# RWKV scan on one core: the outputs of two chunk groups move behind the X and Y products of the second and fourth level in TensorE's order

## The chip, the core and the metric

The kernel runs on one core of a Trainium2 chip. The metric is the device time of one execution in microseconds. Five engines work side by side, each through its own queue in program order: TensorE (PE in the rows; PEld are its weight loads), VectorE (DVE), ScalarE (ACT), GpSimd (POOL) and SyncE (SP). They meet through semaphores alone.

## What is computed

The reference is one encoder layer over two batches (1024 and 256 tokens, 1280 in all). Only its scan matters here. For each of 8 heads of width 64 and for both directions of time it keeps a 64 x 64 state:

```python
def step(S, inp):
    r_t, w_t, k_t, v_t, a_t, b_t = inp
    sa = jnp.einsum('zdhij,zdhj->zdhi', S, a_t)
    S = S * w_t[..., None, :] + sa[..., :, None] * b_t[..., None, :] + v_t[..., :, None] * k_t[..., None, :]
    y = jnp.einsum('zdhij,zdhj->zdhi', S, r_t)
    return S, y
```

The layer around it has an input projection, a neighbourhood attention, a norm of the scan's output per head, a bonus term and a gate, two output projections and a wide MLP. Everything is float32.

## The kernel before, in words

`scan_mixer` (L128) holds the whole scan; the stages before and after it are other functions, each closed by a barrier of all engines. The tokens are cut in chunks of 64 (C); four chunks of both directions are a step (GR = 4 groups g), 5 steps cover the tokens of one tile of two heads, and 4 tiles (ct) make 20 steps. A group g is one chunk of each direction u, for two heads that lie in the two halves of the partitions. The recurrence inside a chunk is solved in closed form: with the Gram products of the step's arrays a triangular matrix is inverted by five doublings, the **levels** l = 0 to 4.

Two groups are in work at once, a **pair** t; 40 pairs and one last round make the loop `for t in range(PAIRS + 1)`, which TensorE, ScalarE and VectorE each run in an order of their own, written out by hand. In pair t, ga and gb are the two groups whose levels are computed (block q = t // 2), sa and sb_ are the two groups of the pair before, whose states and outputs are computed, and sa and sb_ of block qa are the next pair's, for which the Gram products are made. On TensorE:

- `level_q(q, l, g)` (L466): Q = products for level l. It waits until ScalarE has copied X and Y of the level before (`xy_ready`; L810, L813).
- `join` on VectorE (L1046): Q out of PSUM, masked, into `sc_q`. `level_xy` waits for it (`q_ready`).
- `level_xy(q, l, g)` (L478, L482): the new X and Y; at the last level Y alone.
- `state_in`, `solved`, `state_out` (L495 to L524) carry the state from one group to the next, through ScalarE's copies L817 and L821.
- `outputs(qs, g)` (L533, L537, L540): the group's outputs, into their own place in a PSUM bank. `collect` on VectorE (L1056, L1062) takes them out into `sc_y`. The next `state_in` waits until that is done (`y_ready`).
- `gram_products` (L423) and `by_token` (L436, L439, L443) for the next pair. VectorE's `start_group` (`begin` and `turn`: L945, L949, L953, L959) and `mask` (L938) work on the Gram products, each operation waiting for the one before it. `flip` (L452), the last thing of a pair, waits for the mask.

In each pair TensorE goes: level 0, `solved(sa)`, Q of level 1, `state_out(sa)`, `outputs(sa)`, X and Y of level 1, `gram_products(sa)`, `state_in(sb_)`, level 2 with `by_token(sa)`, `state_out(sb_)`, Q of level 3, `outputs(sb_)`, `gram_products(sb_)`, X and Y of level 3, Q of level 4, `by_token(sb_)`, Y of level 4, flips.

VectorE's order is not touched by the change. Its loop has the following lines (L1124 to L1143, cut):

```python
if l == 1 and inner:
    state(qs, sa)
    collect(qs, sa)
...
if l == 3:
    side(t, 2, GRAM_BANK)
    side(t, 1, TOK_BANK)
if l == 3 and inner:
    state(qs, sb_)
    collect(qs, sb_)
if l == 3 and more:
    start_group(qa, sb_)
if l == 4 and more:
    mask(qa, sb_)
```

They stand behind the two joins of level l. At the end of each level below 4, `norm_part` runs a reciprocal (L984) in the blocks with i = q % 5 = 2 (ct > 0) and i = 3 (ct < 3).

**Side work.** In even pairs a step of the norm, bonus or gate of a tile is done beside the levels, in three pieces of 512, 256 and 512 columns: `piece_out` on TensorE puts a piece into a free part of PSUM, `side` on VectorE takes it. One piece uses the bank of the Gram products; `side(t, 3)` on TensorE, directly ahead of `gram_products(qa, sb_)`, waits until VectorE has taken it. The even pairs from 12 to 36, and pair 8, have such pieces. In every second pair ScalarE also computes exponentials for the step after next (`decays`, L759), and POOL prepares the arrays of the next step (L300 to L340, `prepare`).

Of the kernel before, what the change touches and what calls it, by code (L numbers as in the profile page):

```python
# [127 lines left out]
def scan_mixer(nc, lora, params, cn_scan, w_proj, ident, ones, mean, by_heads, by_row, sT, ob, regions, wb, wb_raw,  # L128
               first_kk, first_wl):

    with ExitStack() as ctx:
# [93 lines left out]
        def chunk(u, g):  # L225

            at = (g if u == 0 else GR - 1 - g) * C
            return slice(at, at + C)
# [15 lines left out]
        def fresh(i, u, g):  # L244

            return g == 0 and (i == 0 or i == (NB_P if u == 0 else NB - NB_P))
# [19 lines left out]
        def values(q, u, g):  # L266

            return VT[:, slot(q, u, g), :]

        def nth(q, l, g):  # L270

            return ((q * 2 + g // HALF) * LEVELS + l) * HALF + g % HALF + 1
# [126 lines left out]
        def _(pe):  # L399
# [56 lines left out]
            def level_q(q, l, g):  # L456
                n = q * GR + g
                if l == 0:
                    pe.wait_ge(x1_ready, n + 1)
                    if n >= HALF:  # L460
                        pe.wait_ge(xy_ready, nth(q, 0, g) - HALF)
                else:
                    pe.wait_ge(xy_ready, nth(q, l - 1, g))
                for u in range(2):
                    for rows in heads:
                        last = nc.tensor.matmul(q_out[g][across(rows, u), u, :], AI[g][rows, u, :],  # L466
                                                XY[g][rows, X_AT, u, :], start=True, stop=True)
                last.then_inc(q_ps, 1)

            def level_xy(q, l, g):  # L470
                pe.wait_ge(q_ready, nth(q, l, g))
                if l == 0:
                    pe.wait_ge(flipped, q * 2 + g // HALF + 1)
                if l < LEVELS - 1:
                    for u in range(2):
                        for rows in heads:
                            at = across(rows, u)
                            nc.tensor.matmul(x_out[g][rows, u, :], XY[g][at, Y_AT, u, :], Q1[g][at, u, :],  # L478
                                             start=True, stop=True)
                for u in range(2):  # L480
                    for rows in heads:
                        last = nc.tensor.matmul(y_out[g][rows, u, :], Q1[g][rows, u, :], XY[g][rows, Y_AT, u, :],  # L482
                                                start=True, stop=True)
                last.then_inc(xy_ps, 1)

            def state_in(q, g):
                i, n = q % NB, q * GR + g
                pe.wait_ge(tok_ready, n + 1)
                pe.wait_ge(xy_ready, nth(q, LEVELS - 1, g))
                if n:  # L490
                    pe.wait_ge(s_ready, n)
                    pe.wait_ge(y_ready, n)
                for u in range(2):
                    for rows in heads:
                        last = nc.tensor.matmul(p_out[across(rows, u), u, :], GM[g][rows, u, 2, :],  # L495
                                                values(q, u, g)[rows, :], start=True, stop=fresh(i, u, g))
                for u in range(2):
                    if not fresh(i, u, g):
                        for rows in heads:
                            last = nc.tensor.matmul(p_out[across(rows, u), u, :],  # L500
                                                    AR[q % 2][rows, 0, u, chunk(u, g)],
                                                    S[n % 2][rows, u, :], start=False, stop=True)
                last.then_inc(p_ps, 1)

            def solved(q, g):
                n = q * GR + g
                pe.wait_ge(p_ready, n + 1)
                for u in range(2):
                    for rows in heads:
                        at = across(rows, u)  # L510
                        last = nc.tensor.matmul(u_out[rows, u, :], XY[g][at, Y_AT, u, :], PT[g][at, u, :],
                                                start=True, stop=True)
                last.then_inc(u_ps, 1)
# [14 lines left out]
            def outputs(q, g):  # L528
                i, n = q % NB, q * GR + g
                for u in range(2):  # L530
                    new = fresh(i, u, g)
                    for rows in heads:
                        nc.tensor.matmul(o_out[rows, u, :], values(q, u, g)[rows, :], GM[g][rows, u, 3, :],  # L533
                                         start=True, stop=False)
                    if not new:
                        for rows in heads:
                            nc.tensor.matmul(o_out[rows, u, :], S[n % 2][rows, u, :],  # L537
                                             AR[q % 2][rows, 1, u, chunk(u, g)], start=False, stop=False)
                    for rows in heads:
                        last = nc.tensor.matmul(o_out[rows, u, :], UT[g][rows, u, :], GM[g][rows, u, 1, :],  # L540
                                                start=False, stop=True)
                last.then_inc(y_ps, 1)
# [89 lines left out]
            for t in range(PAIRS + 1):  # L632
                levels, inner, more = t < PAIRS, t > 0, t < PAIRS - 1
                q, ga = t // 2, t % 2 * HALF
                gb = ga + 1
                qs, sa = (t - 1) // 2, (t + 1) % 2 * HALF
                sb_ = sa + 1
                qa = (t + 1) // 2
                ahead = t % 2 == 1 and q + 2 < STEPS
                if levels:  # L640
                    level_q(q, 0, ga)
                    level_q(q, 0, gb)
                if inner:
                    state_in(qs, sa)
                if levels:
                    level_xy(q, 0, ga)
                    level_xy(q, 0, gb)
                if inner:
                    solved(qs, sa)
                if levels:  # L650
                    pe.wait_ge(tok_ready, q * GR + gb + 1)
                side(t, 0)
                if ahead:
                    lora_products(q + 2)
                if levels:
                    level_q(q, 1, ga)
                    level_q(q, 1, gb)
                if inner:
                    state_out(qs, sa)
                    outputs(qs, sa)  # L660
                if levels:
                    level_xy(q, 1, ga)
                    level_xy(q, 1, gb)
                if ahead:
                    pe.wait_ge(ta_ready, q + 3)
                if more:
                    gram_products(qa, sa)
                if inner:
                    state_in(qs, sb_)
                if levels:  # L670
                    level_q(q, 2, ga)
                    level_q(q, 2, gb)
                side(t, 1)
                if more:
                    by_token(qa, sa)
                if inner:
                    solved(qs, sb_)
                if levels:
                    level_xy(q, 2, ga)
                    level_xy(q, 2, gb)  # L680
                if inner:
                    state_out(qs, sb_)
                if more:
                    pe.wait_ge(masked, qa * GR + sa + 1)
                side(t, 2)
                if more:
                    pe.wait_ge(tok_ready, qa * GR + sa + 1)
                side(t, 5)
                if levels:
                    level_q(q, 3, ga)  # L690
                    level_q(q, 3, gb)
                if inner:
                    outputs(qs, sb_)
                side(t, 3)
                if more:
                    gram_products(qa, sb_)
                if levels:
                    level_xy(q, 3, ga)
                    level_xy(q, 3, gb)
                if levels:  # L700
                    level_q(q, 4, ga)
                    level_q(q, 4, gb)
                side(t, 4)
                if more:
                    by_token(qa, sb_)
                if levels:
                    level_xy(q, 4, ga)
                    level_xy(q, 4, gb)
                if t + 1 < PAIRS:
                    flip(qa, sa)  # L710
                    flip(qa, sb_)
# [1712 lines left out]
```

## Time and profile before

| | us |
|---|---|
| three runs, median (lowest to highest) | 2530.23 (2529.64 to 2532.83) |
| profiled execution | 2531.89 |
| its span | 2530.1 |
| TensorE matmul records busy | 2413.9 (95%) |
| VectorE busy | 1150.6 (45%) |
| ScalarE busy | 726.2 (29%) |
| POOL busy | 790.0 (31%) |
| granted TensorE clock, mean | 0.988 |

The time of an execution is 1.8 us more than its span; the profiled one stands 1.7 us above the median. Shares are over the whole span, of which the scan is less than a quarter. Matmul records of this kernel's small tiles overlap, several at a time, so that their number and length do not add up to time; the starts of the weight loads, one for each matmul record, show the order and the pace at which TensorE issues. Idle time in brackets behind a row is that engine's own, and the name behind it is what ended it.

### The profile page before, as it was taken

Reading aid. Unit: us, or ns where it says so; the run is one execution under the profiler, and the core shown is the slowest. Engines: PE = TensorE matmul, PEld = TensorE weight load, DVE = VectorE, ACT = ScalarE, POOL = GpSimd, SP = SyncE. Lnnn points to the kernel's source line nnn. Section 1 sums busy time; section 2 is a strip of 40 time slices with the busy share of each in tenths; the row PEclk is TensorE's granted clock in tenths of the full one; section 3 lists DMA queues with packets and bytes.
Section 4 is the critical chain, followed back from the end, with each engine's and each line's share of the span. In section 5 each row is a group of like instructions: output and inputs, shape, how many; then the busy total and the mean of one; then the engine's idle time right before and its main releaser. Section 6 shows DMA issues by size and latency. Waiting matters only on the chain. (4 is left out here: it accounts for less than half of the span.)

```text
span 2530.1 us, 62968 instructions
## 1 busy us (share of the span) xinstructions
PE 2413.9 (95%) x27732; PEld 2027.7 (80%) x27732; DVE 1150.6 (45%) x2494; ACT 726.2 (29%) x1810; POOL 790.0 (31%) x621
## 2 busy tenths in 40 slices
PE   7999999999998799999999799999999999999997
PEld 6885688888887788878888588888888888888885
DVE  3107820001333566666766554564444444444445
ACT  5117731011111555546455442211100011100014
POOL 3222222222331333333343271043332333232233
PEclk9999999999999999999999999999999999999998
DMA  6201022121111000000000062211100111110114
GB/s 170 51 29 40 10 88 73 69 75 55 34 42 52 3 4 4 4 4 4 4 4 4 3 265 105 98 49 34 42 34 34 51 34 42 43 34 34 36 65 150
DMA packets 39870, 124.92 MB, mean 49 GB/s; under 512 B 11568, under 2 KB 11568, under 8 KB 38448
## 3 DMA queue, kind: packets, MB, share of 16 engines
q1 hardware_dynamic: 39600, 120.90, 14.1%
q8 instruction: 221, 3.62, 0.6%
q14 instruction: 49, 0.40, 0.0%
HBM read 96.24 MB, written 20.97 MB: 46 GB/s over the span
## 5 line engine op out<-in xcount | busy, mean ns | idle before, releaser
L2241 DVE TENSOR_TENSOR ff_f<-ff_f,ff_ps 128x512 f32<-128x512 f32 x300 | 206.0, 687 | 173.1 <-PE ff_ps L98 173.1
L2149 ACT ACTIVATE ff_rl<-ff_ps 128x512 f32<-128x512 f32 (+1 forms) x96 | 50.5, 526 | 748.0 <-PE ff_ps L98 748.0
L2272 DVE TENSOR_TENSOR ff_sq<-ff_rl 128x512 f32<-128x512 f32 (+1 forms) x96 | 124.2, 1294 | 267.6 <-ACT ff_rl L2149 267.3
L1046 DVE TENSOR_TENSOR sc_q<-sc_ps,sc_cs 128x128 f32<-128x128 f32 x400 | 98.5, 282 | 195.5 <-PE sc_ps L466 193.7
L2016 POOL TENSOR_TENSOR ff_wd0h<-ff_wdr,params 128x1024 fp32r<-128x1024 f32 x16 | 30.3, 1893 | 458.5 <-DMA ff_wdr<-in_w_down 341.8
L810 ACT ACTIVATE sc_xy<-sc_ps 128x256 f32<-128x256 f32 x320 | 116.6, 386 | 173.9 <-PE sc_ps L482 171.8
L482 PE MATMUL sc_ps<-sc_xy,sc_q 64*64 64x64 f32 x3200 | 149.8, 220 | 7.6 <-DVE sc_q L1046 6.3
L98 PE MATMUL ff_ps<-hh,ff_wu1h 128*128 128x512 f32 (+1 forms) x384 | 136.0, 354 | 0.0
L98 PE MATMUL ff_ps<-hl,ff_wu1h 128*128 128x512 f32 (+1 forms) x384 | 136.0, 354 | 0.0
L98 PE MATMUL ff_ps<-hh,ff_wu0l 128*128 128x512 f32 (+1 forms) x384 | 135.8, 354 | 0.0
L98 PE MATMUL ff_ps<-hh,ff_wu0h 128*128 128x512 f32 (+1 forms) x384 | 135.8, 354 | 0.0
L98 PE MATMUL ff_ps<-hh,ff_wu1l 128*128 128x512 f32 (+1 forms) x384 | 135.8, 354 | 0.0
L98 PE MATMUL ff_ps<-hl,ff_wu0h 128*128 128x512 f32 (+1 forms) x384 | 135.8, 354 | 0.0
L482 PEld LDWEIGHTS sc_ps<-sc_xy,sc_q 64*64 64x64 f32 x3200 | 126.3, 136 | 10.1 <-DVE sc_q L1046 7.2
L466 PEld LDWEIGHTS sc_ps<-sc_xy,sc_ai 64*64 64x64 f32 x3200 | 76.0, 133 | 63.0 <-issue 29.0
L1820 DVE TENSOR_TENSOR gp_gm<-gp_sg,gp_ps 128x512 f32<-128x512 f32 (+1 forms) x24 | 14.4, 599 | 245.3 <-PE gp_ps L98 245.3
L98 PE MATMUL ff_ps<-ff_wd0h,ff_gh 128*128 128x512 f32 x320 | 124.7, 390 | 1.1 <-DVE ff_f L2243 1.1
L478 PE MATMUL sc_ps<-sc_q,sc_xy 64*64 64x64 f32 x2560 | 119.2, 232 | 6.4 <-DVE sc_q L1046 3.2
L98 PE MATMUL ff_ps<-ff_wd0l,ff_gh 128*128 128x512 f32 x320 | 124.6, 389 | 0.0
L98 PE MATMUL ff_ps<-ff_wd1h,ff_gh 128*128 128x512 f32 x320 | 124.6, 389 | 0.0
L98 PE MATMUL ff_ps<-ff_wd1l,ff_gh 128*128 128x512 f32 x320 | 124.5, 389 | 0.0
L98 PE MATMUL ff_ps<-ff_wd0h,ff_gl 128*128 128x512 f32 x320 | 124.5, 389 | 0.0
(343 smaller groups left out, 6835.3 us busy)
## 6 DMA issues: line engine op xcount, KB each, us to landing
ff_wur<-in_w_up SPq DMA_DIRECT2D x32, 512.0 KB, 3.5
ff_wdr<-in_w_down SPq DMA_DIRECT2D x32, 512.0 KB, 4.2
gwr<-in_w_in SPq DMA_DIRECT2D x31, 512.0 KB, 3.5
gm_dram<-gp_gm SPq DMA_DIRECT2D x8, 1280.0 KB, 4.4
ff_m<-gm_dram SPq DMA_DIRECT2D x16, 640.0 KB, 8.6
fr_x<-in_x SPq DMA_DIRECT2D x10, 512.0 KB, 4.9
ff_xs<-in_x SPq DMA_DIRECT2D x10, 512.0 KB, 4.5
x_dram<-ff_xo SPq DMA_DIRECT2D x10, 512.0 KB, 2.9
```

The costliest lines, as they stand in the source:

```text
L98: mm = nc.tensor.matmul(out, stationary[a], moving[b], start=first and n == 0, stop=last and n == len(pairs) - 1)
L466: last = nc.tensor.matmul(q_out[g][across(rows, u), u, :], AI[g][rows, u, :], XY[g][rows, X_AT, u, :], start=True, stop=True)
L478: nc.tensor.matmul(x_out[g][rows, u, :], XY[g][at, Y_AT, u, :], Q1[g][at, u, :], start=True, stop=True)
L482: last = nc.tensor.matmul(y_out[g][rows, u, :], Q1[g][rows, u, :], XY[g][rows, Y_AT, u, :], start=True, stop=True)
L810: nc.scalar.activation(XY[g][:, :, :, :].rearrange("p n u t -> p n (u t)"), yx_out[g], ACT.Copy).then_inc(xy_ready, 1)
L1046: nc.vector.tensor_tensor(Q1[g][:, :, :], q_out[g], joins[:, l, :].rearrange("p (u t) -> p u t", u=2), ALU.mult).then_inc(q_ready, 1)
L1820: nc.vector.tensor_tensor(gm[c % 2][:, 0, t0:t0 + tn], sga[:, t0:t0 + tn], ps[:, bank(u), 0:tn], ALU.mult).then_inc(merged, 1)
L2016: nc.gpsimd.tensor_tensor(high, w_raw[m], zero_like(high, zero), ALU.add).then_inc(high_done, 1)
L2149: nc.scalar.activation(rl[v % 2][:, 0:tn], ps[:, b, 0:tn], ACT.Relu).then_inc(relu, 1)
L2241: nc.vector.tensor_tensor(own, own, ps[:, 4 + v % 4, :], ALU.add).then_inc(added, 1)
L2272: nc.vector.tensor_tensor(sq[v % 2][:, 0:tn], rl[v % 2][:, 0:tn], rl[v % 2][:, 0:tn], ALU.mult).then_inc(squared, 1)
```

## The change

It moves two calls in TensorE's order within each pair: `outputs(qs, sa)` from ahead of the X and Y products of level 1 to behind them, and `outputs(qs, sb_)` from between the Q products and the Gram products of level 3 to behind the X and Y products of that level, ahead of the Q products of level 4. Nothing else is changed: no instruction is added or taken away, and the orders of VectorE, ScalarE and POOL stay.

```diff
@@ -657,10 +657,11 @@
                     level_q(q, 1, gb)
                 if inner:
                     state_out(qs, sa)
-                    outputs(qs, sa)
                 if levels:
                     level_xy(q, 1, ga)
                     level_xy(q, 1, gb)
+                if inner:
+                    outputs(qs, sa)
                 if ahead:
                     pe.wait_ge(ta_ready, q + 3)
                 if more:
@@ -689,14 +690,14 @@
                 if levels:
                     level_q(q, 3, ga)
                     level_q(q, 3, gb)
-                if inner:
-                    outputs(qs, sb_)
                 side(t, 3)
                 if more:
                     gram_products(qa, sb_)
                 if levels:
                     level_xy(q, 3, ga)
                     level_xy(q, 3, gb)
+                if inner:
+                    outputs(qs, sb_)
                 if levels:
                     level_q(q, 4, ga)
                     level_q(q, 4, gb)
```

## Rows read from the trace of the kernel before

**Rows 1.** Stretches: the scan; busy time and records of each engine, granted clock, DMA.

```profile
837.00:1428.00 591.00, 549.70 (x17192) 481.52 (x17196) 366.42 (x1184) 318.21 (x1005) 206.01 (x254) 0.99 0.02 4
```

**Rows 2.** Groups by line: count, busy us, mean ns, idle before and its releasers.

```profile
L466 PEld LDWEIGHTS sc_ps<-sc_xy,sc_ai 64*64 64x64 f32 x3200 | 76.0, 133 | 63.0 <-issue 29.0 <-ACT sc_xy L810 22.1 <-DVE sc_gm L938 5.3
```

**Rows 3.** Timeline, weight loads, pair 23: start us, length us, engine, line, operation.

```profile
1185.27 0.32 PEld L466 LDWEIGHTS sc_ps<-sc_xy,sc_ai 64*64 64x64 f32 x16 [0.84 <-issue]
1185.50 0.20 PEld L533 LDWEIGHTS sc_ps<-sc_gm,sc_vt 64*64 64x64 f32 x4
...
1186.20 0.85 PEld L423 LDWEIGHTS sc_ps<-sc_ar 64*64 64x64 f32 x16
1186.92 0.35 PEld L478 LDWEIGHTS sc_ps<-sc_q,sc_xy 64*64 64x64 f32 x8
...
1188.12 0.56 PEld L466 LDWEIGHTS sc_ps<-sc_xy,sc_ai 64*64 64x64 f32 x16 [0.27 <-ACT sc_xy L810]
...
1189.76 0.40 PEld L452 LDWEIGHTS sc_ps<-sc_cs,sc_xy 64*64 64x64 f32 x8
1190.39 0.41 PEld L466 LDWEIGHTS sc_ps<-sc_xy,sc_ai 64*64 64x64 f32 x16 [0.23 <-issue]
```

**Rows 4.** Timeline, VectorE, pair 23, from the fourth level's joins on.

```profile
1185.68 0.49 DVE L1046 TENSOR_TENSOR sc_q<-sc_ps,sc_cs 128x128 f32<-128x128 f32 x2 [1.13 <-PE sc_ps L466]
...
1186.47 0.29 DVE L1056 COPY sc_y<-sc_ps 128x128 f32<-128x128 f32 x1
1187.34 0.29 DVE L945 TENSOR_TENSOR sc_gm<-sc_ps,sc_cs 128x128 f32<-128x128 f32 x1 [0.58 <-PE sc_ps L423]
...
1188.56 0.63 DVE L1046 TENSOR_TENSOR sc_q<-sc_ps,sc_cs 128x128 f32<-128x128 f32 x2
1189.10 0.55 DVE L938 TENSOR_TENSOR sc_gm<-sc_ps,sc_cs 128x384 f32<-128x384 f32 x1
```

**Rows 5.** Timelines of VectorE and the weight loads, pair 24, second level.

```profile
1193.60 0.49 DVE L1046 TENSOR_TENSOR sc_q<-sc_ps,sc_cs 128x128 f32<-128x128 f32 x2 [0.67 <-PE sc_ps L466]
...
1196.80 0.29 DVE L1046 TENSOR_TENSOR sc_q<-sc_ps,sc_cs 128x128 f32<-128x128 f32 x1 [1.08 <-PE sc_ps L466]
...
1193.88 0.20 PEld L533 LDWEIGHTS sc_ps<-sc_gm,sc_vt 64*64 64x64 f32 x4
```

**Rows 6.** Timelines of ScalarE and the weight loads, pair 24, third level.

```profile
1195.95 1.28 ACT L759 ACT_TABLE_LOAD   x1
...
1197.78 0.26 ACT L817 ACTIVATE sc_pt<-sc_ps 128x128 f32<-128x128 f32 x1
...
1198.09 0.21 PEld L511 LDWEIGHTS sc_ps<-sc_pt,sc_xy 64*64 64x64 f32 x8 [0.92 <-ACT sc_pt L817]
```

**Rows 7.** Timeline, weight loads, pair 24, fourth level to the flip.

```profile
1202.38 0.85 PEld L423 LDWEIGHTS sc_ps<-sc_ar 64*64 64x64 f32 x16 [0.28 <-DVE sc_bv L1001]
...
1206.16 0.35 PEld L452 LDWEIGHTS sc_ps<-sc_cs,sc_xy 64*64 64x64 f32 x8 [0.18 <-issue]
```

**Rows 8.** Timeline, VectorE, pair 24, from the group's start to the mask.

```profile
1203.52 0.29 DVE L945 TENSOR_TENSOR sc_gm<-sc_ps,sc_cs 128x128 f32<-128x128 f32 x1
...
1204.74 0.51 DVE L984 RECIPROCAL sc_n<-sc_n 96x64 f32<-96x64 f32 x1
1205.17 0.42 DVE L1046 TENSOR_TENSOR sc_q<-sc_ps,sc_cs 128x128 f32<-128x128 f32 x2
1205.51 0.54 DVE L938 TENSOR_TENSOR sc_gm<-sc_ps,sc_cs 128x384 f32<-128x384 f32 x1
```

**Rows 9.** Timelines of POOL and VectorE, pair 28, the same place.

```profile
1263.88 1.29 POOL L308 TENSOR_TENSOR sc_ar<-sc_fac,sT 128x512 f32<-128x512 f32 x1
...
1263.98 1.33 DVE L953 TENSOR_TENSOR sc_xy<-sc_ai,sc_cs 128x128 f32<-128x128 f32 x1
```

**Rows 10.** Pair 37's last Y products in the timeline, and the stretch behind it.

```profile
1402.37 0.54 PEld L482 LDWEIGHTS sc_ps<-sc_xy,sc_q 64*64 64x64 f32 x16 [2.31 <-DVE sc_q L1046]
...
1403.50:1406.90 3.40, 3.34 (x99) 3.16 (x97) 0.91 (x4) 1.96 (x7) 0.00 (x0) 0.50 0.00 0
```

## The prediction

> **What bounds the kernel now.** Three views, in this order. First the stretches: the scan runs from 837 to 1428 us, and in these 591 us the matmul records cover 550 us while VectorE is busy 366 us [rows 1]. A busy TensorE is no proof of a bound here, because small matmuls overlap. So next the groups by line, read for the idle time ahead of the weight loads: the loads of L466 (`level_q`) sat idle 63.0 us in all, 22.1 us of it ended by ScalarE's copy L810 [rows 2]. Last the timelines of two pairs, which show where in a pair that idle time is and what VectorE does meanwhile. I number the pairs by the loop variable t (0 to 40); t = 23 stands for a plain pair, t = 24 for one with side work. A pair takes 591/40 = 14.8 us on average.
>
> In pair 23 [rows 3, 4] the weight loads of the fourth level go: Q products at 1185.27, outputs 1185.50, Gram products 1186.20, X and Y products 1186.92, Q products of the fifth level 1188.12. X and Y issue in about 0.82 us, so 1188.12 - 1186.92 - 0.82 = 0.38 us is a stall, and L810 ends it. That is the hole which moved outputs would fill. VectorE meanwhile collects the outputs (L1056, 1186.47), waits for the Gram products, and from 1187.34 runs `start_group` for the next group; the join of the fifth level starts at 1188.56 and the mask L938 at 1189.10, ending 1189.65. The flip goes at 1189.76, 0.11 us later. VectorE is thus already the last to arrive at the flip.
>
> **The change, part by part.** It adds and removes no instruction. It moves 24 matmul records of outputs (20 or 16 where a state is fresh) twice in each pair. Nothing of POOL's or SP's queue is moved. No wait is added on TensorE, but VectorE's own order is not changed: in it `collect` stands ahead of `start_group`, which stands ahead of the fifth level's join. Queued behind `collect`'s wait for the outputs are therefore the group's four operations, that join, the mask, and behind them TensorE's last Y products and the flip.
>
> *Move 1, second level.* In pair 24 the joins start at 1193.60; the first takes about 0.30 us and is seen by TensorE some 0.06 us later, so at 1193.96 [rows 5]. State products end their issue at 1193.88, where the outputs now start. X and Y would go at 1193.96 or so, outputs behind them: +0.06 us in each of 38 pairs, +2.3 us. The second join is ready before the second group's products are due. The collected outputs come 0.65 us later on VectorE, which sat idle 1.08 us before the third level's join, and the next `state_in`, which needs them, stands behind 0.72 us of Gram products against 0.30 + 0.29 us for the collection: about 0.1 us to spare, so nothing. If that cover were gone it would cost up to 0.3 us a pair. There is a gain: ScalarE copies X and Y 0.6 us earlier, so the table load behind them starts earlier too. In pair 24 that load (1.28 us from 1195.95) and the exponential hold the copy L817 back to 1197.78, and TensorE's L511 goes only at 1198.09, after 0.92 us of idle time [rows 6]. Six such pairs (2, 12, 14, 22, 24, 34) get back 0.58 us each: -3.5 us. Move 1 together: -1.2 us, bounds -4 and +10.
>
> *Move 2, fourth level, in a plain pair* (16 of the 38: 1 to 5, 9, 10, 11, 13, 19, 21, 23, 29, 31, 33, 38) [rows 3, 4]. Gram products start at 1185.50 instead of 1186.20. The joins of this level start at 1185.68 and end by 1186.17; Gram's 0.72 us covers them, and X and Y go at 1186.22. Outputs follow at 1187.04 and issue for 0.70 us; the fifth level's Q products go at 1187.74 instead of 1188.12. So 0.38 us is gained on TensorE. On VectorE: the last load of the outputs is at 1187.72, the collection starts 0.30 us behind it as before (1186.17 to 1186.47), at 1188.02, and `start_group` 0.21 us later, at 1188.23 instead of 1187.34. That is **+0.89 us**. From `start_group` to the join it took 1188.56 - 1187.34 = 1.22 us, a chain of four dependent operations which nothing shortens, so the join starts at 1189.45, the mask ends at 1190.54 and the flip goes at 1190.65 against 1189.76. Of the 0.89 us, 0.38 us was idle anyway: the next pair's first Q products went at 1190.39, 0.38 us after the flip's issue, held by ScalarE's last copies. They now go right behind the flip. Price of a plain pair: 0.89 - 0.38 = 0.51 us, and 16 x 0.51 = 8.2 us.
>
> *With reciprocals* (7 pairs: 6, 7, 15, 17, 25, 27, 35). A reciprocal L984 of 0.51 us stands between `start_group` and the join, which starts when it is done [rows 8]; there flip and next pair follow VectorE without slack. All 0.89 us count: 6.2 us.
>
> *With a side piece* (pairs such as 24). Gram products wait there for VectorE to have taken a piece out of the Gram bank (1202.38, released by L1001) [rows 7]. They can't start earlier; the outputs only hid that wait. So X and Y keep their place too, and outputs end their issue at 1202.38 + 0.72 + 0.82 + 0.70 = 1204.62. Collection 1204.90, `start_group` 1205.11 against 1203.52 [rows 8]: **+1.59 us**. With a reciprocal (14, 16, 24, 26, 34) all of it counts, since the flip at 1206.16 waits for the mask: 5 x 1.59 = 8.0 us. Without one (12, 20, 22, 30, 32, 36) I take off the 0.38 us of the plain pair: 6 x 1.21 = 7.3 us.
>
> *Pairs where POOL holds the group back* (8, 18, 28, 37). In pair 28 VectorE's L953 took 1.33 us instead of 0.29, and ended 0.1 us after POOL's L308 [rows 9]. If it ends when POOL ends, a later start is partly absorbed: `start_group` would reach L949 at 1264.80, be held to 1265.2, and then have L953 yet to do, 0.3 to 0.9 us behind before. I take 0.6: 4 x 0.6 = 2.4 us; the bounds are 0 and 1.59 each. The Trainium skill (SBUF — State Buffer, Who interferes with whom) says that a VectorE instruction with two SBUF inputs and a GpSimd instruction that reads SBUF exclude each other, the later one blocking fully. L949 and L953 have such inputs. Were it a plain slowdown instead, the four pairs would cost 6.4 us and not 2.4, and the sum would be 4 us higher.
>
> **The sum.** Move 2: 8.2 + 6.2 + 8.0 + 7.3 + 2.4 = 32.1 us. Move 1: -1.2 us. Together +30.9 us. The profiled execution took 2531.9 us (span 2530.1), so its like would be 2562.8 us. It stood 1.7 us above the median of the three runs, 2530.2; from the median the forecast is 2561 us. What follows the scan waits for the scan and is shifted whole.
>
> **The rivals.** *The hole is filled and VectorE has room* (faster). If `collect` did not hold the fifth level's join back, for instance because the group's work were ready before that join is wanted, each of 38 pairs would keep the 0.38 us of ScalarE's stall: 14.4 us, and move 1's 1.2 us: 2530 - 16 = 2515 us. For it: 22.1 us of waiting for L810 are in the table [rows 2] and VectorE is 38% idle in the scan. Against it: the turned group ended at the very time the join began. It decides at a spare of 0.9 us on VectorE ahead of the flip in plain pairs and 1.6 us in the others; the rows show 0.1 to 0.4. Chance 0.07. *Gain and loss cancel*, if a pair's delay were mostly taken up by waits that I did not see: within 5 us of 2530. Chance 0.05. *The delay counts and the clock falls as well.* In pair 37 TensorE sat 2.31 us before L482, and behind that the granted clock was 0.50, the lower level of 1.2 GHz, for a stretch of 3.4 us [rows 10]. At half speed a stretch of 3.4 us costs at most 1.7 us; TensorE waits in part of it anyway, and my estimate is 1.2 us. After the change the five pairs at +1.59 would have a stall of 0.2 + 1.6 = 1.8 us there and the six others with a piece about 1.3 us. Pairs 8, 18 and 28 have such stalls of 1.3 us now without a fall. If all eleven fell: 11 x 1.2 = 13 us, 2574 us. Chance 0.15. *My chain as worked out*: 0.73. Within it a lag of 0.1 us misjudged in each of 38 pairs is 4 us, the held pairs are 4 us either way, and the plain pairs' 0.38 us of slack taken off wrongly is 6 us on the high side; if other waits take up twice what I allow, 13 us fall on the low side.
>
> **How the numbers follow.** Forecast 2561 us. Range 2544 to 2579 us: 17 us below for more slack than I see, 18 us above for the clock. About a tenth lies under it, with the two rivals that end there. A change of 0.2% is about what a measurement of this kernel can tell from none. Faster by over 0.2%: 0.07. Within 0.2%: 0.05. Slower by over 0.2%: 0.88.
>
> **What would show it.** In the profile after: L466's idle time behind L810 falls by about 10 us (right); before the fifth level's Y products (L482) there is a new idle time of TensorE ended by VectorE's L1046, some 0.5 us in plain pairs and 1.6 us in those with a piece (right). VectorE's L1056 and L1062 show idle time ended by the outputs L540 of 20 us and more, and `start_group`'s L945 hardly any ended by L423. I am wrong if the fifth level's join starts in pair 23 as long after the fourth level's Q products as before, 3.29 us [rows 3, 4] (1188.56 - 1185.27); I expect 4.2 us, and in pair 24 5.6 us. If the granted clock shows new stretches at 0.5 inside the scan, the third rival has come.

## The result

| | us, median (lowest to highest) | |
|---|---|---|
| before | 2531.5 (2529.6 to 2537.6), 4 runs | |
| after | 2577.8 (2571.1 to 2582.8), 4 runs | ratio 1.0182, 95% interval 1.0169 to 1.0196 |

The change makes the kernel slower by 46 us. The forecast was 2561 us, 31 us more than before, with a range of 2544 to 2579. The direction and the mechanism were right, and the loss was 15 us larger than forecast: the median lies 1 us under the upper end of the range. The profiled execution after has a span of 2577.3 us, and the scan alone is 47 us longer than before; the stages around it kept their time.

The groups by line of the kernel after, whose columns are those of [rows 2]. VectorE's and ScalarE's lines are one higher than before (L1047 is the join, L1057 and L1063 are `collect`, L946, L950, L954, L960 `start_group`, L939 the mask):

```profile
L482 PEld LDWEIGHTS sc_ps<-sc_xy,sc_q 64*64 64x64 f32 x3200 | 130.9, 141 | 53.4 <-DVE sc_q L1047 51.9 <-issue 1.3
L466 PEld LDWEIGHTS sc_ps<-sc_xy,sc_ai 64*64 64x64 f32 x3200 | 76.1, 137 | 43.2 <-issue 25.2 <-ACT sc_xy L811 10.4 <-DVE sc_gm L939 6.1
L946 DVE TENSOR_TENSOR sc_gm<-sc_ps,sc_cs 128x128 f32<-128x128 f32 x80 | 22.5, 281 | 3.2 <-PE sc_ps L423 3.2
L1057 DVE COPY sc_y<-sc_ps 128x128 f32<-128x128 f32 x40 | 11.7, 291 | 48.3 <-PE sc_ps L540 48.3
L1063 DVE TENSOR_TENSOR sc_y<-sc_y,sc_ps 128x128 f32<-128x128 f32 x40 | 11.5, 287 | 49.2 <-PE sc_ps L540 49.1
```

About half of the hole that the outputs were to fill is gone: idle time behind ScalarE's copy fell from 22.1 us [rows 2] to 10.4 us. In its place the loads of L482 now sit idle 53.4 us, 51.9 us of it ended by VectorE's join; before, the same loads sat idle 10.1 us. And VectorE itself waits 97 us for outputs (L540) with `collect`, where it waited 6 us before, while `start_group` (L946), queued behind it, waits 3.2 us for its Gram products instead of 14.6 us.

Pair 23 after, weight loads and then VectorE, answers to [rows 3] and [rows 4]:

```profile
1212.23 0.32 PEld L466 LDWEIGHTS sc_ps<-sc_xy,sc_ai 64*64 64x64 f32 x16 [0.84 <-issue]
1213.16 0.85 PEld L423 LDWEIGHTS sc_ps<-sc_ar 64*64 64x64 f32 x16 [0.61 <-ACT sc_n L782]
1213.88 0.35 PEld L478 LDWEIGHTS sc_ps<-sc_q,sc_xy 64*64 64x64 f32 x8
...
1214.73 0.20 PEld L533 LDWEIGHTS sc_ps<-sc_gm,sc_vt 64*64 64x64 f32 x4
...
1215.38 0.37 PEld L466 LDWEIGHTS sc_ps<-sc_xy,sc_ai 64*64 64x64 f32 x16
...
1217.41 0.54 PEld L482 LDWEIGHTS sc_ps<-sc_xy,sc_q 64*64 64x64 f32 x16 [0.97 <-DVE sc_q L1047]
1218.14 0.35 PEld L452 LDWEIGHTS sc_ps<-sc_cs,sc_xy 64*64 64x64 f32 x8 [0.18 <-issue]
1218.39 0.39 PEld L466 LDWEIGHTS sc_ps<-sc_xy,sc_ai 64*64 64x64 f32 x16
```

```profile
1212.64 0.49 DVE L1047 TENSOR_TENSOR sc_q<-sc_ps,sc_cs 128x128 f32<-128x128 f32 x2 [1.13 <-PE sc_ps L466]
...
1215.69 0.29 DVE L1057 COPY sc_y<-sc_ps 128x128 f32<-128x128 f32 x1 [2.18 <-PE sc_ps L540]
1215.90 0.28 DVE L946 TENSOR_TENSOR sc_gm<-sc_ps,sc_cs 128x128 f32<-128x128 f32 x1
...
1217.10 0.45 DVE L1047 TENSOR_TENSOR sc_q<-sc_ps,sc_cs 128x128 f32<-128x128 f32 x2
1217.48 0.54 DVE L939 TENSOR_TENSOR sc_gm<-sc_ps,sc_cs 128x384 f32<-128x384 f32 x1
```

Read downwards: the fifth level's Q products follow the outputs without a gap (1215.38), then TensorE idles 0.97 us before its last Y products. VectorE sat 2.18 us in `collect`'s wait, and `start_group` began 0.21 us behind it. The flip goes 0.12 us after the mask's end, as before. Pair 24 after, both engines, answers to [rows 7] and [rows 8]:

```profile
1228.53 0.32 PEld L466 LDWEIGHTS sc_ps<-sc_xy,sc_ai 64*64 64x64 f32 x16 [0.76 <-issue]
1229.82 0.85 PEld L423 LDWEIGHTS sc_ps<-sc_ar 64*64 64x64 f32 x16 [0.96 <-DVE sc_bv L1002]
...
1234.47 0.54 PEld L482 LDWEIGHTS sc_ps<-sc_xy,sc_q 64*64 64x64 f32 x16 [1.61 <-DVE sc_q L1047]
...
1232.56 0.28 DVE L946 TENSOR_TENSOR sc_gm<-sc_ps,sc_cs 128x128 f32<-128x128 f32 x1
...
1234.19 0.42 DVE L1047 TENSOR_TENSOR sc_q<-sc_ps,sc_cs 128x128 f32<-128x128 f32 x2
```

`start_group` begins 2.74 us behind the Gram products' first load; before it was 1.14 us [rows 7, 8]. That is 1.60 us more; the forecast was 1.59. The fifth level's join comes 5.66 us behind the fourth level's Q products (5.6 forecast). But the mean granted clock of the scan fell. The stretch of the scan after, with the columns of [rows 1]:

```profile
837.00:1475.00 638.00, 554.99 (x17200) 492.22 (x17200) 366.41 (x1184) 321.81 (x1006) 206.12 (x254) 0.96 0.02 4
```

0.96 against 0.99 before. The record of the granted clock holds eleven stretches at 0.50 between the scan's start and its tail, 41 us long together; before there were two, 6.8 us long.

### The profile page after: what moved, and what is told of

The parts are those of the page before. It is cut to its first block and busy times, and to the rows that moved or that the text cites. A ratio compares the mean times of both kernels' runs of the same rounds, so it can differ in the third digit from the quotient of the medians.

```text
span 2577.3 us, 62967 instructions
## 1 busy us (share of the span) xinstructions
PE 2420.0 (94%) x27732; PEld 2039.0 (79%) x27732; DVE 1155.8 (45%) x2494; ACT 729.4 (28%) x1810; POOL 790.8 (31%) x621
## 5 line engine op out<-in xcount | busy, mean ns | idle before, releaser
L482 PE MATMUL sc_ps<-sc_xy,sc_q 64*64 64x64 f32 x3200 | 156.2, 226 | 46.7 <-DVE sc_q L1047 46.4
L482 PEld LDWEIGHTS sc_ps<-sc_xy,sc_q 64*64 64x64 f32 x3200 | 130.9, 141 | 53.4 <-DVE sc_q L1047 51.9
L1047 DVE TENSOR_TENSOR sc_q<-sc_ps,sc_cs 128x128 f32<-128x128 f32 x400 | 96.6, 280 | 162.2 <-PE sc_ps L466 161.2
L478 PE MATMUL sc_ps<-sc_q,sc_xy 64*64 64x64 f32 x2560 | 120.5, 238 | 10.1 <-DVE sc_q L1047 7.4
L98 PE MATMUL ff_ps<-ff_wd1h,ff_gl 128*128 128x512 f32 x320 | 124.5, 389 | 0.0
```

Source lines behind the costliest of these rows:

```text
L98: mm = nc.tensor.matmul(out, stationary[a], moving[b], start=first and n == 0, stop=last and n == len(pairs) - 1)
L1047: nc.vector.tensor_tensor(Q1[g][:, :, :], q_out[g], joins[:, l, :].rearrange("p (u t) -> p u t", u=2), ALU.mult).then_inc(q_ready, 1)
```

## The experiments

My theory: VectorE's queue order (`collect` ahead of `start_group`) carries the loss, POOL makes it larger in some pairs, and the lower clock adds to it. The rival: the outputs' new place on TensorE costs by itself. All ratios below are against runs of the kernel before on the same chip, with the 95% interval. For lengths of pairs I take the starts of the first Q product of successive pairs in the two profiles.

### Each move alone

```diff
                     state_out(qs, sa)
-                    outputs(qs, sa)
                 if levels:
                     level_xy(q, 1, ga)
                     level_xy(q, 1, gb)
+                if inner:
+                    outputs(qs, sa)
```

> The kernel before with the first of the two moves alone: outputs(sa) behind the X and Y products of the second level. If my terms for it hold (+0.06 us in 38 pairs, -0.58 us in the six pairs where ScalarE's table load holds a copy back), it takes 2530 us, 1 us less than before, a ratio of 0.9995, and at most one stretch at the lower clock more than before. If this move carries a good part of the 46 us, for instance through the later collection on VectorE, it takes 2540 us or more.

Measured: 2531.4 us, ratio 0.9997 (0.9988 to 1.0006): no change that can be told from none. In the profile the median pair is 0.06 us longer, as forecast. Of the six pairs that the forecast names for the gain, five (12, 14, 22, 24, 34) are 0.38 to 0.72 us shorter, where 0.52 us was forecast, and pair 2 is 0.12 us longer.

```diff
-                if inner:
-                    outputs(qs, sb_)
                 side(t, 3)
                 if more:
                     gram_products(qa, sb_)
                 if levels:
                     level_xy(q, 3, ga)
                     level_xy(q, 3, gb)
+                if inner:
+                    outputs(qs, sb_)
```

> The kernel before with the second move alone: outputs(sb_) behind the X and Y products of the fourth level. If the whole loss is this move's, it takes 2578 to 2580 us, ratio 1.019, with the same stalls before the last Y products as the kernel after (1.08 us in plain pairs, 1.7 us with a reciprocal, 2.8 us and more in pairs 8, 18, 28, 37) and about ten stretches at the lower clock inside the scan. If the two moves only cost what they do together, it is nearer to before, under 2560 us.

Measured: 2576.4 us, ratio 1.0177 (1.0163 to 1.0191), nine stretches at the lower clock. The loss is the second move's alone.

### The cause: what stands behind the collection

On the kernel after, VectorE's loop:

```diff
                     if l == 3 and inner:
                         state(qs, sb_)
-                        collect(qs, sb_)
                     if l == 3 and more:
                         start_group(qa, sb_)
                     if l == 4 and more:
                         mask(qa, sb_)
+                    if l == 4 and inner:
+                        collect(qs, sb_)
```

> The kernel after, with one change on VectorE: collect(sb_) goes from ahead of start_group to behind the mask of the last level. The outputs stay where the change put them on TensorE. If VectorE's order is the cause, everything comes back and some of the 0.38 us of ScalarE's stall with it: plain pairs and those with a reciprocal gain 0.38 us (23 x 0.38 = 8.7 us), pairs with a piece lose 0.3 us where there is no reciprocal (6 x 0.34 = 2 us), move 1 gives 1 us: 2524 us, ratio 0.997, and no more stretches at the lower clock than before. If instead the outputs' place on TensorE costs (other products drawn apart, the clock), it stays at 2560 us or more.

Measured: 2530.1 us, ratio 0.9993 (0.9982 to 1.0003). TensorE's order is that of the kernel after, and the whole 46 us is gone. Pair 23 of this run, weight loads and VectorE:

```profile
1184.47 0.37 PEld L466 LDWEIGHTS sc_ps<-sc_xy,sc_ai 64*64 64x64 f32 x16
...
1185.45 0.55 PEld L482 LDWEIGHTS sc_ps<-sc_xy,sc_q 64*64 64x64 f32 x16
...
1183.39 0.29 DVE L946 TENSOR_TENSOR sc_gm<-sc_ps,sc_cs 128x128 f32<-128x128 f32 x1 [0.79 <-PE sc_ps L423]
...
1184.94 0.49 DVE L1047 TENSOR_TENSOR sc_q<-sc_ps,sc_cs 128x128 f32<-128x128 f32 x2 [0.26 <-PE sc_ps L466]
1185.35 0.55 DVE L939 TENSOR_TENSOR sc_gm<-sc_ps,sc_cs 128x384 f32<-128x384 f32 x1
1185.81 0.28 DVE L1057 COPY sc_y<-sc_ps 128x128 f32<-128x128 f32 x1
```

`start_group` waits for its Gram products again, the join waits for TensorE and not the other way, and L482 shows no wait. The rival falls: the outputs' new place on TensorE costs nothing that can be measured once nothing waits behind their collection. The expected gain (2524 us) was not measured: ten of the 16 plain pairs were shorter, mostly by 0.4 to 0.6 us (0.38 us forecast), the six with side work of ScalarE or POOL were 0.1 to 0.3 us longer, and this profile has seven stretches at the lower clock, 24 us long, and pairs 16, 17, 26 and 27, where some of them lie, are 0.9 to 2.6 us longer than before.

The same edit, and nothing else, on the kernel before, as a control:

> The kernel before with only VectorE's collect(sb_) behind the last level's mask, TensorE's order as before. A control for the run with both. If that step in VectorE's order is worth nothing by itself, since start_group waits for the Gram products there anyway, it takes 2531 us, within 0.2%. If VectorE's queue was a bound before (piece pairs, where start_group follows the collection without idle time), it is 2 to 5 us faster: 13 pairs x 0.2 us = 2.6 us and less contention with POOL.

Measured: 2530.8 us, ratio 0.9997 (0.9988 to 1.0006). By itself the edit is worth nothing; it is worth 46 us where the outputs come late.

### A smaller dose

```diff
-                if inner:
-                    outputs(qs, sb_)
                 side(t, 3)
                 if more:
                     gram_products(qa, sb_)
+                if inner:
+                    outputs(qs, sb_)
                 if levels:
                     level_xy(q, 3, ga)
```

> The kernel before with outputs(sb_) moved half way: behind the Gram products of the fourth level but still ahead of its X and Y products. A smaller dose of the same cause. By VectorE's queue: in plain pairs the Gram products end 0.70 us earlier and the collection comes 0.7 us later than before, just as start_group would begin, so nothing (+0.06 us); in pairs with a piece, where the Gram products cannot start earlier, the outputs put everything behind them back by 0.7 to 0.8 us: 11 pairs x 0.75 = 8 us, the four held pairs 1 to 2 us each, 12 to 14 us in all, 2545 us, ratio 1.005. If the place of the outputs behind the X and Y products is what costs, this takes 2532 us.

Measured: 2546.9 us, ratio 1.0060 (1.0047 to 1.0073), 15 us. By classes of pairs, median: plain 0.0 us, with a piece 0.72 us, with piece and reciprocal 0.90 us, held pairs 1.43 us. Its pair 24:

```profile
1208.74 0.85 PEld L423 LDWEIGHTS sc_ps<-sc_ar 64*64 64x64 f32 x16 [0.96 <-DVE sc_bv L1001]
1209.56 0.25 PEld L533 LDWEIGHTS sc_ps<-sc_gm,sc_vt 64*64 64x64 f32 x4
...
1210.58 0.29 DVE L1056 COPY sc_y<-sc_ps 128x128 f32<-128x128 f32 x1 [0.91 <-PE sc_ps L540]
1210.79 0.28 DVE L945 TENSOR_TENSOR sc_gm<-sc_ps,sc_cs 128x128 f32<-128x128 f32 x1
```

`start_group` comes 2.05 us behind the Gram products' first load, against 1.14 us before. The loss follows the time of the collection, pair class by pair class. This profile, too, has seven stretches at the lower clock, 24 us long, so that a part of the 15 us can be the clock's; the medians of the classes depend on it less.

### POOL in the held pairs

In pair 28 of the kernel after (16.2 us before, 19.4 us now) VectorE, POOL and the weight loads read:

```profile
1300.99 1.36 DVE L950 TENSOR_TENSOR sc_ai<-sc_gm,sc_cs 128x128 f32<-128x128 f32 x1
1302.38 1.23 DVE L954 TENSOR_TENSOR sc_xy<-sc_ai,sc_cs 128x128 f32<-128x128 f32 x1
...
1300.93 1.27 POOL L322 TENSOR_TENSOR sc_ar<-sc_ar,sc_neg 128x512 f32<-128x512 f32 x1
1302.15 1.31 POOL L324 TENSOR_TENSOR sc_ar<-sc_ar,sc_neg 128x512 f32<-128x512 f32 x1
...
1304.19 0.54 PEld L482 LDWEIGHTS sc_ps<-sc_xy,sc_q 64*64 64x64 f32 x16 [2.71 <-DVE sc_q L1047]
```

Each of VectorE's two operations ends 0.15 us after one of POOL's, and they take 1.36 and 1.23 us instead of 0.29. Before, these two of POOL ran after `start_group`, and only L306 and L308 met it (0.74 and 1.33 us in pair 28). The experiment, on the kernel after:

```diff
-                    pool.wait_ge(x1_ready, (q - 1) * GR + 3)
+                    pool.wait_ge(x1_ready, (q - 1) * GR + 4)
```

> The kernel after, with one wait of POOL changed: its two multiplications of a step's arrays by the inverse decays wait for the block's last turn instead of the last but one, so that they can't run beside start_group. By the theory that in pairs 8, 18 and 28 these operations hold VectorE's L950 and L954 (1.35 and 1.23 us instead of 0.29), those become short, the stall before the last Y products there falls from 2.8 to about 1.3 us, and with it go most stretches at the lower clock near these pairs: 3 x 1.5 us and 3 to 5 us of clock, 2568 us. If POOL has no part in it, 2577 us as after; if POOL is then late for the next step's Gram products, more.

Pair 28 of that run:

```profile
1299.01 0.29 DVE L950 TENSOR_TENSOR sc_ai<-sc_gm,sc_cs 128x128 f32<-128x128 f32 x1
1299.33 0.29 DVE L954 TENSOR_TENSOR sc_xy<-sc_ai,sc_cs 128x128 f32<-128x128 f32 x1
...
1300.12 1.27 POOL L322 TENSOR_TENSOR sc_ar<-sc_ar,sc_neg 128x512 f32<-128x512 f32 x1 [1.72 <-DVE sc_xy L960]
```

With POOL's two out of the way both take 0.29 us, and TensorE's stall before the last Y products falls from 2.71 to 1.21 us. So the hold is POOL's. As a total the run is inconclusive: 2572.8 us (2561.7 to 2578.1), ratio 1.0157 (1.0137 to 1.0178), 5 us less than after with overlapping intervals. Pair 8, with one stretch at the lower clock instead of two, became 1.8 us shorter than in the profile after. Pair 28 became 1.7 us longer: 10.2 us of it are at the lower clock there instead of 3.8 us. In all, eight stretches took 37.5 us in this profile.

### The clock

In the kernel after, first the stretch behind pair 28's stall, then the one ahead of it:

```profile
1304.80:1308.20 3.40, 3.33 (x82) 3.17 (x80) 0.50 (x2) 1.71 (x7) 2.35 (x7) 0.50 0.03 5
1297.99:1301.40 3.41, 3.41 (x84) 3.41 (x80) 0.90 (x3) 0.77 (x2) 3.27 (x4) 0.50 0.00 0
```

0.50 is the lower of the two levels, 1.2 GHz, with 80 weight loads in 3.4 us; an equal stretch at full speed in the kernel before, from 1188.0 on, holds 109. The first begins 0.6 us behind TensorE's stall of 2.71 us. The second begins 1.1 us behind a wait of 1.02 us ahead of the Gram products, and it makes the later stall longer: X, Y and outputs run at the lower clock, the collection comes later, and POOL's next operations are met. To take the clock out, matmuls that nobody uses were put into stalls, into unused columns of a PSUM bank, on the kernel after. First in six pairs:

```diff
+            def fill(q, n, bank):
+                x = AR[q % 2]
+                for k in range(n):
+                    rows, u = heads[k % 2], k // 2 % 2
+                    nc.tensor.matmul(ps[rows, bank, 4 * C:5 * C], x[rows, 0, u, 0:C],
+                                     x[rows, 0, u, 0:C], start=True, stop=True)
...
+                if t in (8, 18, 28, 37):
+                    pe.wait_ge(s_ready, qs * GR + sb_ + 1)
+                    fill(q, 32, U_BANK)
                 if levels:
                     level_xy(q, 4, ga)
```

and 48 records, `fill(q, 24, P_BANK)`, ahead of the fourth level's X and Y products in pairs 17 and 27.

> The kernel after, with small matmuls into unused columns of a PSUM bank in the longest stalls of six pairs: 64 records (1.9 us) ahead of the last Y products in pairs 8, 18, 28 and 37, 48 records (1.4 us) ahead of the fourth level's X and Y products in pairs 17 and 27. They compute nothing that is used. They take TensorE no time that it had other work for. If the stretches at the lower clock carry a part of the loss by themselves, most of the eleven go and 5 to 10 us come back: 2570 us. If the loss is delay on VectorE alone and the clock follows from it at no cost, it stays at 2577 us.

Measured: 2572.2 us, ratio 1.0161 (1.0148 to 1.0174). Five of the expected 5 to 10 us came, with an interval that overlaps that of the kernel after, and the clock was not held: eight stretches, 34 us, two of them in pairs that had none in the kernel after (15 and 36). Half a test. So all stalls were filled:

```diff
+                if t in (11, 17, 21, 27, 31):
+                    fill(q, 16 if t in (11, 21) else 32, P_BANK)
...
+                if t >= 2 and t % 2 == 0 and has_side(*side_step(t)):
+                    fill(q, 14, P_BANK)
                 side(t, 3)
...
+                recip = q % NB in (2, 3) and 3 <= q <= 17
+                if 1 <= t < PAIRS - 1:
+                    pe.wait_ge(s_ready, qs * GR + sb_ + 1)
+                    fill(q, 40 if t in (8, 18, 28, 37) else 24 if recip else 14, U_BANK)
                 if levels:
                     level_xy(q, 4, ga)
```

> The kernel after, with small unused matmuls in nearly all the stalls that it has in the second half of a pair: 28 records ahead of the last Y products in plain pairs, 48 where a reciprocal stands, 80 in pairs 8, 18, 28 and 37; 28 ahead of the fourth level's Gram products where a piece is waited for; 32 or 64 ahead of the X and Y products in pairs 11, 17, 21, 27, 31. They are meant to hold the granted clock. By the pairs that had no stretch at the lower clock, the delay through VectorE and POOL is about 35 us and the clock the rest: with the clock held 2567 us, ratio 1.014, and fewer than four stretches at the lower clock in the scan. If the clock's stretches cost nothing of their own, 2577 us with the clock held. If the fillers themselves are late, above 2577 us.

Measured: 2563.7 us, ratio 1.0124 (1.0110 to 1.0138). The scan's stretch in its profile:

```profile
837.00:1462.00 625.00, 602.16 (x19368) 540.71 (x19368) 360.71 (x1180) 320.62 (x1006) 205.84 (x254) 1.00 0.02 4
```

The granted clock is at its upper level from 843 us on; only the scan's first 5 us are at the lower one. TensorE has 2168 matmul records more to do in 13 us less. Pair 28 of this run (L965 and L969 are L950 and L954 of the kernel after):

```profile
1289.12 0.53 DVE L965 TENSOR_TENSOR sc_ai<-sc_gm,sc_cs 128x128 f32<-128x128 f32 x1
1289.68 0.64 DVE L969 TENSOR_TENSOR sc_xy<-sc_ai,sc_cs 128x128 f32<-128x128 f32 x1
...
1290.13 1.32 POOL L322 TENSOR_TENSOR sc_ar<-sc_ar,sc_neg 128x512 f32<-128x512 f32 x1
```

L969 begins ahead of POOL's L322 now, where in the kernel after L950 met L322 and L954 met L324. With the clock held the change costs 1.24% of 2530 us = 31 us; the other 0.58%, 15 us, came with the lower clock, its knock-on through the later collection included. Fillers cannot tell those two apart. Both figures are good to about 2 us. In pairs 8, 18 and 28 the fillers were themselves late (the last Y products go 0.77 to 0.82 us behind the join's start, elsewhere mostly 0.31 us), which is 1.4 us there and 0.8 us in other pairs; and the kernel before, which both are compared with, has two stretches of its own. The four runs of the kernel after agree, without any filler: 2582.8 us at a mean granted clock of 0.978, 2579.2 at 0.980, 2576.4 at 0.981 and 2571.1 at 0.985. Their line, 1.7 us for each 0.001, leads to about 2562 us at the 0.990 of the filled runs, an estimate.

### Versions that keep the gain

The late collection, with `outputs(sb_)` left where it was in the pairs in which TensorE waits there for side work:

```diff
+                early = (t % 2 == 0 and t >= 2 and has_side(*side_step(t))) or (t % 2 and t // 2 % NB == 1 and t // 2 >= NB)
+                if inner and early:
+                    outputs(qs, sb_)
                 side(t, 3)
...
-                if inner:
+                if inner and not early:
                     outputs(qs, sb_)
```

> Both moves with the late collection as in the run e3_both_moves_collect_late, but outputs(sb_) stays ahead of the Gram products in those pairs where TensorE waits there for side work (even pairs with a piece, and pairs 13, 23, 33), since it hides that wait. Against that run the piece pairs get back 0.3 us each and plain pairs keep their 0.38 us: 2526 us, ratio 0.997 of before, if the granted clock does not take it back; with the clock falling seven times in the scan as in that run, about 2530 us.

Measured: 2527.9 us, ratio 0.9986 (0.9978 to 0.9995).

To this the edit of POOL's wait shown above (`+ 3` to `+ 4`):

> The run e8_selective_collect_late (both moves, collection behind the mask, outputs left in place where TensorE waits for side work) with POOL's two multiplications waiting for the block's last turn. If POOL holding VectorE's group start in pairs 8, 18 and 28 cost 1.3 us a pair (the stall before the last Y products there, 1.3 us in the kernel before), it gives back 4 us: 2524 us, ratio 0.997. If POOL's later end delays the next Gram products, nothing or a loss: 2528 us or more.

Measured: 2525.4 us, ratio 0.9982 (0.9973 to 0.9991). Expected were 4 us over the run above; 1 us came, less than the intervals tell. In its profile the group's start in pairs 8, 18 and 28 still meets L306 and L308 (0.71 to 0.75 us and 1.34 us), since `outputs` stay ahead there.

The same edit of POOL's wait alone, on the kernel before:

> The kernel before with that wait of POOL alone. The share of e10 that has nothing to do with the moved outputs: 3 x 1.3 = 4 us, 2528 us, ratio 0.9985, if POOL's hold on VectorE is what costs in pairs 8, 18, 28 of the kernel before as well; no change if TensorE was not waiting for it.

Measured: 2530.6 us, ratio 1.0002 (0.9994 to 1.0011). A miss of mine, and its profile says why: L949 and L953 still take 0.71 to 1.34 us in pairs 8, 18 and 28, because there L306 and L308 are what they meet [rows 9], and those did not move.

Last the version with late collection, selected outputs and POOL's wait, with fillers (`fill` as above):

```diff
+                if t in (17, 27):
+                    fill(q, 24, P_BANK)
                 if levels:
                     level_xy(q, 3, ga)
                     level_xy(q, 3, gb)
...
+                if t in (8, 18, 28, 37):
+                    pe.wait_ge(s_ready, qs * GR + sb_ + 1)
+                    fill(q, 32 if t == 37 else 18, U_BANK)
                 if levels:
                     level_xy(q, 4, ga)
```

> The run e10_selective_pool_waits with small unused matmuls in its longest stalls: 36 records ahead of the last Y products in pairs 8, 18 and 28, 64 in pair 37, 48 ahead of the fourth level's X and Y products in pairs 17 and 27. That run had three stretches at the lower clock in the scan, 10 us long in all. If each costs about what it did in the kernel after (15 us for eleven, 1.3 us each) and the fillers hold the clock, 2521 us, ratio 0.9967. If those stretches fall in elsewhere, in the side work, 2525 us as without.

Measured: 2524.7 us beside 2533.3 us for the kernel before on that chip, ratio 0.9963 (0.9949 to 0.9976), with one stretch at the lower clock in the scan instead of three. It has the lowest ratio of all and beats both kernels, by 9 us against the one before; its interval overlaps that of the run without fillers, so that their own share is not shown.

## Why the prediction was right, and where it was short

In the table, the pairs' classes: forecast for both moves (move 1 put to the pairs that it names), the profile after, and the profile with the clock held, in us summed over the class against the profile before. Single pairs scatter by up to 1 us, since each profile has a few stalls of that size that no wait explains ("issue"), in other pairs each time.

| class | pairs | forecast | after | clock held |
|---|---|---|---|---|
| plain | 16 | 8.6 | 13.5 | 11.8 |
| with reciprocal | 7 | 6.6 | 10.2 | 7.7 |
| with piece | 6 | 6.5 | 4.3 | 4.7 |
| piece and reciprocal | 5 | 6.6 | 7.3 | 5.8 |
| held by POOL | 4 | 2.6 | 10.9 | 3.8 |
| all (with pair 0) | | 30.9 | 46.6 | 34.0 |

- **What bounds it, and the queue.** Right. The collection ahead of `start_group` gates the last join, and VectorE, not TensorE, sets the flip. Both moves with the late collection show it: the same TensorE order without the loss.
- **Move 1.** Not contradicted: -1.2 us forecast, 0.9997 measured, which its interval can't tell from -1.2 us or from nothing.
- **Pairs with a piece or a reciprocal.** Right. With the second move alone the median pair with piece and reciprocal was 1.60 us longer (1.59 forecast), with piece alone 1.07 us (1.21), with reciprocal alone 0.95 us (0.89). With both moves the pairs with a piece alone came to 4.3 us and not 6.5; in the runs with one move each they fall short by 1.1 us in the second move (6.2 us against 7.3) and by 1.3 us in the first (-2.1 us against -0.8), most of it in pair 36.
- **Plain pairs.** Undersized, 0.51 us against a median of 0.83 us. I took pair 23 as typical without asking what its outputs hid. In pairs 13, 23 and 33 they hid TensorE's wait for ScalarE's square root: the Gram products of pair 23 show it now, 0.61 us ended by L782. So the fifth level's join came 4.87 us behind the fourth level's Q products, where I had said 4.2. In pairs 11, 21 and 31 POOL's bonus product (2.9 us) holds VectorE's L926, the fourth level's joins are late, and the X and Y products could not move up; TensorE's idle time ahead of them grew from 0.25 to 0.94 us (pairs 11, 21). With the second move alone these six pairs were 0.88 to 1.05 us longer. Pairs 9, 19 and 29 were 1.6 to 1.9 us longer for another reason: the lower clock behind the stall of the pair before reaches into them. With the clock held they were 0.4 to 0.8 us longer.
- **The held pairs.** 2.4 us were forecast for the second move and 10.9 us measured with both moves, but what was missing is the clock and not POOL. With all stalls filled, pairs 8, 18 and 28 were 1.1 to 1.3 us longer, of which 0.5 us is the fillers' own lateness; that leaves 0.6 to 0.9 us, where I had said 0.6. With the second move alone pair 8, which had no stretch at the lower clock there, was 0.69 us longer; pairs 18 and 28, which had, were 6.4 and 4.2 us longer. L954 took 1.23 to 1.25 us in each of the seven cases with such a stretch just ahead (pairs 8, 18 and 28 after, 18 and 28 with the second move alone, 8 and 18 with the first fillers) and 0.64 us in each of the five without. So L322 and L324 are met in turn only where the lower clock has first made the collection later still. That the Trainium skill's rule is a mutual exclusion (SBUF — State Buffer, Who interferes with whom) fits these rows: an operation of 0.29 us ended 0.15 us behind POOL's, whichever POOL operation that was, and returned to 0.29 us when POOL was moved. Such a lock absorbs a delay only as long as the delay doesn't reach the other engine's next operation.
- **The clock.** The term that was missing from the sum. The forecast left it out and gave it a chance of 0.15 with 13 us and 2574 us. It came, with 15 us. The place was mostly wrong: I expected falls behind stalls of 1.8 us before the last Y products in pairs with a piece. Of the eleven stretches four begin at such a stall, but at the stalls of 2.7 to 2.9 us in pairs 8, 18, 28 and 37. Two follow a wait of 2.33 us for the fourth level's join in pairs 17 and 27 (1.63 us before). Of the other five, four begin 0.2 to 1.1 us behind the wait ahead of the Gram products in pairs 8, 16, 18 and 28. That wait is 1.02 us now and was 0.33 us: the outputs had hidden the rest. Only the fifth, behind the stall of 1.6 us at the end of pair 26, is of the kind that I expected. With the clock held the loss is 31 us, the forecast's 30.9; that closeness is partly luck, since plain pairs were too low and piece pairs too high.
- **Faster or unchanged.** The hole was half filled, as that rival says (22.1 to 10.4 us of waiting for L810), but VectorE had no 0.9 us to spare.

What stays open: how much of the 15 us is the lower clock itself and how much is what it delays. That an execution without the fillers can have more or less of the lower clock shows in the spread, 11.7 us between the fastest and the slowest run after. And why the run with both moves and the late collection had seven stretches at the lower clock was not tested by itself. Four of them (pairs 16, 26, 28, 36) begin within 1.1 us behind a wait of 1.02 us ahead of the Gram products; the run that leaves the outputs there, with waits of 0.33 us, had none of these four and two stretches in all. But pairs 8, 18, 20 and 30 had the same wait and no fall, and each is one profile: that is argued, not shown.

## What to carry to other kernels

Before moving a producer in one engine's order, find the wait for it on the consumer's engine and read what is queued behind that wait: here 0.3 us of copying held a chain of 1.2 us, and moving the consumer with the producer turned 46 us lost into nothing. Ask of a block that is moved away what waits it hid, class of step by class of step, since a typical step doesn't show them. Here four of the eleven stretches at the lower clock began just behind such a wait. And read the neighbour engine's next few operations, not only the one that overlaps now: a larger delay meets them.

## What the runs showed of the hardware that I had not expected

VectorE operations with both inputs in SBUF (L950, L954) took 1.36 and 1.23 us instead of 0.29 us beside POOL's multiplications, one for one, and 0.29 us again with these moved. L926, with one input in SBUF, took 2.89 us instead of 0.42 us beside POOL's bonus product. The granted clock fell to 0.50 far more readily than I had allowed: eleven times in the scan after, four times at a stall of 2.7 to 2.9 us, but in pairs 8, 16, 18 and 28 where TensorE had only been idle for 1.0 us just before. It did not fall behind each such wait: pairs 20, 30 and 36 of the same profile had one and no stretch. And with 2168 extra matmul records the kernel was 14 us faster (2577.8 to 2563.7 us), in a scan whose clock stayed at its upper level but for the first 5 us.
